# A decoder step with paged decode attention: decay rows over 128 partitions, a new token's decay as a bias, copies before memsets, and the first product in two halves

## The reference

```python
c_all = jnp.cumsum(jnp.concatenate([past_logf, logf_new], axis=1), axis=1)
cq = c_all[:, past_len:]
s = jnp.einsum('bqhd,bkhd->bhqk', qi, k) * scale
s = s + ci[..., None] - ckt[:, :, None, :]          # + cq[t] - c[s], per head
s = jnp.where(k_pos[None, :] <= pi[:, None], s, MASK_VALUE)
p = jax.nn.softmax(s, axis=-1)
o = jnp.einsum('bhqk,bkhd->bqhd', p, v)
```

## Time and profile before

| | |
|---|---|
| three runs | 1964.43, 1966.2, 1970.72 us; median 1966.2 |
| the profiled execution | 1965.43 us, of which the span from first to last instruction is 1963.4 |
| granted TensorE clock, mean | 0.975 of full speed |
| busy, share of the span | PE 95%, PEld 87%, DVE 47%, ACT 35%, POOL 29% |
| stages | layer 0 from 0; prompt attention from about 1010; decode from 1128; last trunk from 1475 |
| the 16 DMA engines, mean over the span | 139 GB/s; in decode 388 to 394 GB/s |

### The profile page before, as it was taken

How to read it: one execution, slowest core, us unless ns; L and a number is a source line. 1 busy time by engine, 2 the same in 40 slices (tenths; PEclk the granted TensorE clock), 3 DMA queues, 4 the chain that set the end, 5 groups by cost and what they waited for, 6 DMA issues and landing times. The chain is left out here.

```text
span 1963.4 us, 39366 instructions
## 1 busy us (share of the span) xinstructions
PE 1857.2 (95%) x16353; PEld 1698.7 (87%) x16353; DVE 928.5 (47%) x1406; ACT 690.0 (35%) x1082; POOL 578.0 (29%) x275
## 2 busy tenths in 40 slices
PE   6999998999999999999979899888889999999998
PEld 5999997999999999999977666555549999999998
DVE  4757767355555500354648654433323455555000
ACT  4355455332222121355436643333323312212121
POOL 2323322243333433333346200000003333334332
PEclk9999999999999999999998899999889999999999
DMA  4232241222222333222243789999983222223322
GB/s 109 82 105 78 78 111 48 83 79 86 86 77 86 92 85 88 59 73 76 76 143 104 250 283 393 394 391 388 389 329 86 87 82 80 86 82 92 88 76 78
DMA packets 288853, 272.92 MB, mean 139 GB/s; under 512 B 19234, under 2 KB 249859, under 8 KB 288036
## 3 DMA queue, kind: packets, MB, share of 16 engines
q1 hardware_dynamic: 286740, 267.91, 42.3%
q10 hardware_dynamic: 1792, 1.44, 0.2%
q0 software_dynamic: 144, 1.05, 0.2%
HBM read 252.09 MB, written 14.08 MB: 136 GB/s over the span
## 5 line engine op out<-in xcount | busy, mean ns | idle before, releaser
L2033 POOL TENSOR_TENSOR a_wl<-a_wraw,a_wh 128x1024 fp32r<-128x1024 f32 (+2 forms) x91 | 233.8, 2569 | 410.6 <-ACT a_wh L1959 410.6
L2033 POOL TENSOR_TENSOR b_wl<-b_wraw,b_wh 128x1024 fp32r<-128x1024 f32 (+1 forms) x67 | 175.4, 2619 | 300.6 <-ACT b_wh L1959 300.6
L1915 PE MATMUL ps<-xh,a_wh 128*128 128x288 f32 x1104 | 238.1, 297 | 0.0
L1915 PE MATMUL ps<-xl,a_wh 128*128 128x288 f32 x1104 | 237.0, 296 | 0.0
L1915 PE MATMUL ps<-xh,a_wl 128*128 128x288 f32 x1104 | 236.7, 296 | 0.0
L1959 ACT ACTIVATE a_wh<-a_wraw 128x1024 fp32r<-128x1024 f32 (+2 forms) x91 | 100.6, 1106 | 338.8 <-PE ps L1915 319.0
L1959 ACT ACTIVATE b_wh<-b_wraw 128x1024 fp32r<-128x1024 f32 (+1 forms) x67 | 76.0, 1134 | 318.4 <-PE ps L1915 318.4
L1915 PEld LDWEIGHTS ps<-xh,a_wh 128*128 128x128 f32 x1104 | 177.1, 187 | 1.1 <-issue 0.2
L1915 PEld LDWEIGHTS ps<-xh,a_wl 128*128 128x128 f32 x1104 | 177.2, 187 | 0.6
L1915 PEld LDWEIGHTS ps<-xl,a_wh 128*128 128x128 f32 x1104 | 177.2, 187 | 0.6
L2051 DVE TENSOR_TENSOR xT<-xT,ps 128x576 f32<-128x576 f32 x32 | 24.1, 754 | 322.0 <-PE ps L1915 322.0
(11 more groups left out here) (347 smaller groups left out, 3863.0 us busy)
## 6 DMA issues: line engine op xcount, KB each, us to landing
sa_kp<-in_cache_k SPq DMA_DIRECT2D x128, 512.0 KB, 11.1
sa_vp<-in_cache_v SPq DMA_DIRECT2D x102, 512.0 KB, 14.6
a_wraw<-in_w_gate_up SPq DMA_DIRECT2D x44, 512.0 KB, 3.8
b_wraw<-in_w_gate_up SPq DMA_DIRECT2D x44, 512.0 KB, 3.7
a_wraw<-in_a_w_in SPq DMA_DIRECT2D x32, 512.0 KB, 4.2
a_wraw<-in_w_down SPq DMA_DIRECT2D x16, 704.0 KB, 4.7
xl_plain<-in_cache_v SPq DMA_DIRECT2D x22, 512.0 KB, 14.9
b_wraw<-in_w_down SPq DMA_DIRECT2D x16, 704.0 KB, 4.7
```

The source lines that it names most:

```text
L1915: mm = pe.matmul(ps[0:width(n), bank(n) + a, 0:HALF], wt[:, base(n) + t, 0:width(n)], ap[:, first + t, a * HALF:(a + 1) * HALF], start=kin ...
L2033: pool.tensor_tensor(part(wl, n), part(wraw, n), part(wh, n).bitcast(F32), ALU.subtract).then_inc(e["low"], 1)
```

## The change

1. **Decode, rows.** `neg_decay` becomes `[sequence*16+head, part, token]`, so that a sequence's 256 KB are one piece. One DMA lays it on 128 partitions of 512 tokens (partition = head*8 + part*4 + group). A new constant `c_rowsel` (256 KB, loaded into `pp` at the beginning of decode and rounded by ScalarE into `rowsel`) has for each group a 128 x 128 matrix that picks the rows of this group and head. The matmul L1502 has 128 partitions in place of 34.
2. **Decode, bias.** The new tokens' decay isn't a row of the matmul any more. It is stored once, unsplit, and loaded as a column for each sequence into `shift` (128 x 8) by eight DMAs of single elements (`load_shift`) in prompt attention at j = 6, between `parts(6)` and three key pages. `save` adds it as the bias of its activation, `tail` with a tensor_scalar, and the maximum of the tail is taken from the result. The memsets of the ones, of `rowl`, half of the split of the new decay (two small VectorE instructions) and the waits on them go.
3. **Prompt attention.** VectorE makes its two copies ahead of its two memsets. ScalarE alternates: query half, copy, query half, copy.
4. **Layer 0.** Chunk 4 goes to bank 2 and waits for `low` at 2. The first product is made by halves of the tokens: the 24 matmuls of the first half wait for three chunks, those of the second for five.

```diff
@@ FirstNorm.tensor
             if c == 4:
-                pe.wait_ge(self.low, 1)
+                pe.wait_ge(self.low, 2)
...
+    def bank(self, c):
+        return 2 * c if c < 4 else 2
@@ hgrn_layer, unit
                     if n == 0:
-                        pe.wait_ge(first.low, 5)
-                    for t in range(KD):
-                        for i, (wt, at) in enumerate(((wh, k.xh), (wh, k.xl), (wl, k.xh))):
-                            for a in range(2):
...
+                        pe.wait_ge(first.low, 3)
+                    for half in ((0,), (1,)) if n == 0 else ((0, 1),):
+                        if half == (1,):
+                            pe.wait_ge(first.low, 5)
+                        for t in range(KD):
+                            for i, (wt, at) in enumerate(((wh, k.xh), (wh, k.xl), (wl, k.xh))):
+                                for a in half:
...
@@ prompt_attention
                     if j == 6:
+                        past.load_shift(sp)
                         keypages.load_early(sp, 5, 8)
...
-                for a in range(2):
-                    query_high(0, a)
-                past.act_rows(act)
+                query_high(0, 0)
+                past.act_rows(act, 1)
+                query_high(0, 1)
+                past.act_rows(act, 3)
...
+                past.dve_rows(dve, 0)
+                past.dve_rows(dve, 2)
                 dve.memset(qb[DH:DH + 4, 0].bitcast(F32), 1.0).then_inc(ones[0], 1)
-                past.dve_rows(dve, 0)
                 dve.memset(kb[DH:DH + 4, 0].bitcast(F32), 1.0).then_inc(ones[0], 1)
-                past.dve_rows(dve, 2)
@@ PastDecay
+    def load_shift(self, sp):
+        sp.wait_ge(self.newstored, 32)
+        for c in range(4):
+            for a in range(2):
+                at = a * DH + c * 2 * NQ
+                sp.dma_start(self.shift[32 * c + 16 * a:32 * c + 16 * a + 16, :], self.k.new_decay[:, at:at + 2 * NQ].rearrange("b n -> n b"),
+                             allow_slow_non_contiguous=True).then_inc(self.shifted, 16)
@@ sample_attention, rows
-                    s = b % 2
-                    for part in range(2):
-                        sp.dma_start(rowr[part * BH:(part + 1) * BH, s, :].bitcast(F32), k.neg_decay[part, b * BH:(b + 1) * BH, :]
-                                     ).then_inc(rload[s], 16)
-                    new_row(b)
...
+                    sp.dma_start(rowr[:, b % 2, :].bitcast(F32), k.neg_decay[b * BH:(b + 1) * BH].rearrange("h s (g n) -> (h s g) n", g=G)
+                                 ).then_inc(rload[b % 2], 16)
...
-                sp.wait_ge(past.newstored, 32)
-                sp.wait_ge(e["cleared"], 1)
+                sp.dma_start(pp[:, 0:G, :], k.w["c_rowsel"]).then_inc(e["sel"], 16)
                 rows(0)
@@ sample_attention, scores
-                            pe.wait_ge(rload[s], b // 2 * 64 + 64)
-                            pe.wait_ge(e["ones"], 3)
+                            pe.wait_ge(rload[s], b // 2 * 16 + 16)
+                            pe.wait_ge(e["selected"], 1)
...
-                        pe.matmul(ps[:, group % 2, :], rowl[:, s, :], rowr[:, s, g * SEQ:(g + 1) * SEQ], start=True, stop=False,
+                        pe.matmul(ps[:, group % 2, :], rowsel[:, g, :], rowr[:, s, :], start=True, stop=False,
@@ sample_attention, scalar
-                    act.activation(pr[:, b % 2, g * SEQ:(g + 1) * SEQ], ps[:, group % 2, :], ACT.Copy).then_inc(e["saved"], 1)
+                    act.activation(pr[:, b % 2, g * SEQ:(g + 1) * SEQ], ps[:, group % 2, :], ACT.Identity, bias=past.shift[:, b:b + 1]
+                                   ).then_inc(e["saved"], 1)
...
+                act.wait_ge(past.shifted, 128)
...
+                    if n == 0:
+                        act.wait_ge(e["sel"], 16)
+                        act.activation(rowsel[:], pp[:, 0:G, :], ACT.Copy).then_inc(e["selected"], 1)
@@ sample_attention, vector
-                    dve.tensor_copy(stail[:], ring_bank(n)[:, 0:NQ]).then_inc(e["tailed"], 1)
-                    dve.tensor_reduce(mx[:, G:G + 1], ring_bank(n)[:, 0:NQ], AX.X, ALU.max).then_inc(e["tailed"], 1)
+                    dve.tensor_scalar(stail[:], ring_bank(n)[:, 0:NQ], past.shift[:, b:b + 1], None, ALU.add).then_inc(e["tailed"], 1)
+                    dve.wait_ge(e["tailed"], 2 * b + 1)
+                    dve.tensor_reduce(mx[:, G:G + 1], stail[:], AX.X, ALU.max).then_inc(e["tailed"], 1)
```

More of the change, by code:

```diff
@@ L1203, in room @@
         self.cum2, self.cnew = k.sb(st, "pd_cum", [P, 2, NQ]), k.sb(st, "pd_cnew", [P, 2, NQ])
[L1204 removed]
+        self.newparts = k.sb(st, "pd_newparts", [P, 2, NQ], F32R)
     def load(self, sp):
@@ L1253, in quarter, with act_rows @@
         return ap[:, g * SEQ:(g + 1) * SEQ]
[L1255 to L1259, removed]
+    def act_rows(self, act, g):
+        act.wait_ge(self.turned, g + 1)
+        dst, src = self.spread(g)
+        act.activation(dst, src, ACT.Copy).then_inc(self.arows, 1)
     def act_high(self, act, g):
@@ L1318, in dve_new @@
         dve.wait_ge(self.cum, 3)
-        for part in range(2):
[L1320 to L1324, removed]
+        dve.tensor_copy(self.newparts[:, 0, :], self.cnew[:, 1, :]).then_inc(self.newparted, 1)
+        dve.wait_ge(self.newparted, 1)
+        dve.tensor_tensor(self.newparts[:, 1, :], self.cnew[:, 1, :], self.newparts[:, 0, :].bitcast(F32), ALU.subtract
+                          ).then_inc(self.newparted, 1)
 def sample_attention(k, ks, qs, oT, past, keypages, valuepages, room):
@@ L1331, in sample_attention @@
     e = {n: k.sem("sa_" + n) for n in (
-        "const", "fixed", "ones", "cleared", "filled", "scored", "saved", "mx", "max", "exp", "sum", "inv", "queries", "tailed",
-        "vnew", "mixed", "om", "picked", "done", "newrows")}
+        "const", "fixed", "filled", "scored", "saved", "mx", "max", "exp", "sum", "inv", "queries", "tailed",
+        "vnew", "mixed", "om", "picked", "done", "newrows", "sel", "selected")}
     copied = {n: k.sem("sa_copied_" + n) for n in ("act", "dve")}
@@ L1619, in _ @@
                 act.wait_ge(past.headed, 16)
-                for s in range(2):
-                    act.activation(rowl[0:2 * BH, s], past.headrow, ACT.Copy).then_inc(e["fixed"], 1)
+                act.activation(rowl[:], past.headrow, ACT.Copy).then_inc(e["fixed"], 1)
+                act.wait_ge(past.shifted, 128)
                 for n in range(BLOCKS * NB + PROB_AT + 1):
@@ L1639, in _ @@
             def _(pool):
-                pool.memset(rown[2 * BH:2 * BH + 2].bitcast(F32), 1.0).then_inc(e["ones"], 1)
-                for s in range(2):
-                    pool.memset(rowr[2 * BH:2 * BH + 2, s].bitcast(F32), 1.0).then_inc(e["ones"], 1)
                 raw, high, low = (r[:, 0:KD, :] for r in k.ring)
@@ L1723, in _ @@
                         if n < 2:
-                            dve.wait_ge(e["fixed"], 3)
+                            dve.wait_ge(e["fixed"], 2)
                             queries(n)
@@ L2433, in program @@
                 row_stored = k.sem("rows_stored")
-                past = PastDecay(k, past_logf, room[:, D + 2 * P:], pages, room[0:2 * BH, D + P:D + 2 * P])
+                past = PastDecay(k, past_logf, room[:, D + 2 * P:], pages, room[0:2 * BH, D + P:D + 2 * P], gains["a_norm"])
                 heads = AttentionInputs(k, row_stored, past)
```

42 lines of the change are left out of this document (18 added, 24 removed).

## The result

Seven runs of the changed kernel gave a median of 1953.65 us (1951.08 to 1960.91), beside 1966.2 for the kernel before: ratio 0.9934, 95% interval 0.9916 to 0.9953, so 13.0 us. A second measurement of the same kernel, later, gave 1959.05 us in twelve runs (1952.39 to 1963.54) and 0.9955 (0.9940 to 0.9969), 8.8 us. The change makes the kernel faster; by how much is known to some 4 us. The profiled execution took 1951.08 us, with a span of 1949.3 (before: 1965.43 and 1963.4).

A forecast was written before the change was run, and what follows sets the result against it. It took TensorE to bound the products, waits between engines prompt attention, and held DMA engines decode; 9.6 + 0.9 + 1.2 + 3.4 = 15.1 us off 1965.4 gave 1950.3, with 0.8 for the median 1951.1 us, range 1944 to 1959.

The forecast's parts named there:

- The row load: Decode: rows on 2 x 16 partitions cost 1.9 us a sequence beyond their bytes; 9.6 us saved for b = 3 to 7.
- the rival on descriptors: Decode row loads: cost goes by descriptors, so 128 pieces are slower than before, 1990 us; chance 0.03.
- take over half of the saving: Decode rival: TensorE becomes the bound and half of the 9.6 us is lost, 1956 us; chance 0.12.
- Decode's beginning: First scores of decode: rows arrive at 1133.0, scores at 1133.3; 0.9 us gained.
- the half clock behind it: Transposes behind decode's first wait: a bound of 1.6 us more if their half clock goes; not in the sum.
- the load of b = 2: Decode: this row load falls before the DMA engines are the bound; taken as 0, at most another 2.3 us.
- Waits for keys: Decode: TensorE's waits for key pages would shrink from 30 to about 20 us.
- Layer 0: First product starts at 23.7, not 25.49, and runs at full clock; done at 30.2 instead of 33.6, 3.4 us gained.
- Prompt attention: Its beginning: sums start at 1016.6 instead of 1017.82, 1.2 us gained; up to 3 more if the half clock goes.
- the rival that I gave 0.04: Prompt attention: the shift loads hold up head pair 7; at 4 us lost, 1955 us; chance 0.04.
- my 1104.4: Prompt attention: when SP gets past shift loads, key pages and `decays(7)`, ahead of `parts(7)` at 1104.60; cost nothing.
- The sum: Whole kernel: 9.6 + 0.9 + 1.2 + 3.4 = 15.1 us gained, median 1951.1 us.

The follow-up runs named there:

- rows128_512b: The changed kernel with each 2 KB of decay rows cut into four 512 B pieces by gaps in DRAM, still on 128 partitions; 1954.34 us in one run.
- pages_last: Changed kernel, shift loads in SP's gaps, pair 5's parts ahead of stores and pages, early key pages 2, 3, 3 behind pairs 5, 6, 7; 1949.87 us.
- changed_again: The changed kernel once more, word for word, on the same chip beside pages_last; 1959.05 us, 0.9955 to the kernel before.
- no_decode: The kernel before with only the reordered prompt attention and the first product by halves, decode as before; 1963.91 us, 0.9979.
- pages_behind: The changed kernel with the last four key pages before decode issued behind the selection constant and first rows; 1955.75 us, 0.9933.

## Why the prediction was right, and where it wasn't

*The row load.* Right in cause, and near in size. I took 1.5 + 1.6 + 2.0 + 2.3 = 7.4 us for b = 3 to 6; from issue to issue it is 173.1 - 166.6 = 6.5. Behind the issue of b = 7 decode is 2.8 us shorter (105.98 and 103.13), where I had 2.2. The rows on 32 partitions apart show the cause, and rows128_512b puts the rival on descriptors out. TensorE didn't take over half of the saving either.

*Decode's beginning.* Undersized. From the first transposes to sequence 3's issue it is 66.4 us in place of 68.6, so 2.2, where I took 0.9. The wait itself shrank by 0.23 only: I had the arrival at 1133.0, 4.9 us behind the first transposes, and it came after 5.8. But the half clock behind it, which I kept as a bound, went (1.3 us). The other 0.7 us have no row. All of it is there when `rows(2)` is issued (31.4 us behind the first transposes before, 29.1 after), so the load of b = 2 gave nothing, as in the sum. Decode in all gave 11.55 against 10.5.

*Waits for keys.* I wrote that they would go from 30 to about 20 us; they are 25 to 30 in the traces with the new layout. The step that failed is that the saving would show as less idle time. From the issue of sequence 3's rows to that of sequence 7's, 6.5 us shorter, TensorE's idle time falls from 22.2 to 20.6 us and its busy time from 150.9 to 146.0. The time at half clock falls from 17 to 14 us, which is worth at most 1.7 us of busy time. What the other 3.2 us are stays open.

*Layer 0.* The step is right: the first product gets the full clock, and it is out at 30.1 to 31.2 in eleven traces against 33.6 in two, 2.5 to 3.5 us where I took 3.4. I took the start for 23.7; it was 24.51 here and 23.50 in pages_last. Here TensorE's 31 transposes ahead of it took 4.99 us, in the kernel before 3.93 from the same start, and I have no reason for it. The twelfth trace with the halves, changed_again, is the late one told above. At the last head the median of the same eleven is 301.4 against 304.1 in two: 2.7 us of the 3.4 are left. In the changed kernel's own trace it is 1.3; no_decode, with the same layer 0, has 2.6, so I take it for scatter.

*Prompt attention.* The 1.2 us came exactly (3.39 us to the sums in place of 4.57), and the half clock stayed, as in the sum. It was then lost again, by the rival that I gave 0.04: the shift loads hold up head pair 7. In the eight traces with the loads where the change puts them it waits 0.3 to 3.0 us (median 2.0), in the others with pages as before not at all. I had reckoned SP's time, and that held: the eight loads took 4.74 us in place of 3.9, but the parts of pair 6 were out 2.6 us sooner, and those of pair 7 at 1102.83, before my 1104.4. What I left out is the queue behind SP. The three pages used to be issued 7.4 us ahead of these parts, and now 3.7, and 1.5 MB at 407 GB/s take 3.9 by my estimate: the parts land when the pages have.

*The sum.* The typical pieces, 2.7 in layer 0, 1.2 - 2.0 in prompt attention and 11.5 in decode, make 13.4 us where I had 15.1. The times say 13.0 and 8.8. That the first median, 1953.65, lies within 3 us of my 1951.1 is in part luck: too little at decode's beginning and the loss at head pair 7, which I had at nothing, cancel in part, and the median of twelve more runs of the same kernel lies 5 us higher. That what layer 0 wins reaches the end is seen for both early parts together (no_decode, 4.1 us), not for the halves alone, since the scatter below is larger than they are.

## What to carry to other kernels

Where the DMA engines are the bound, look for stretches with full share and few GB/s: here a transfer of 256 KB to 2 x 16 neighbouring partitions cost 0.64 + 1.9 us, four times its bytes at 407 GB/s. Most of that fell on the pages beside it, and every fourth partition was as good as all 128. A DMA that costs nothing in the queue that issues it can still push a large transfer closer ahead of a small, urgent one; reckon the bytes in flight when the urgent one is issued. And when pages only change places ahead of one waiter or another, the gain is what the last of them leaves.

## What the runs showed of the hardware

The time from the last V of layer 0 to the gather runs the same code in every kernel and took 698.4 to 706.0 us. In the two that lie furthest apart, 7.4 of the 7.6 us arise in one place, between 318 and 385 us. TensorE stands with nothing to wait for that the profile shows ("issue") ahead of the small matmuls of the last head. In the longer case this stall is longer, and the granted clock is lower behind it, but also before it (0.50 from 318 to 320 us, 1.00 in the other). The first is no_decode, the second pages_behind:

```profile
323.85 0.46 PE L394 MATMUL ps<-hg_levels 128*32 128x64 f32 x14 [1.84 <-issue]
...
330.00:340.00 10.00, 9.29 (x92) 8.66 (x91) 5.54 (x15) 6.20 (x10) 0.00 (x0) 1.00 0.22 61
```

```profile
326.76 0.46 PE L395 MATMUL ps<-hg_levels 128*32 128x64 f32 x14 [3.55 <-issue]
...
330.00:340.00 10.00, 10.00 (x40) 6.84 (x41) 5.70 (x21) 3.66 (x7) 0.00 (x0) 0.58 0.03 9
```

From 385 us on the two run in step, 7.2 us apart. Why the instructions come late in some executions stays open, as does why the wait ahead of pair 5 is anything from 3.3 to 8.5 us. The two together are as large as the spread of 10 us and more between runs of one kernel. That they make it isn't shown, since only one run of each has a trace. A spread of this size hides whatever is worth 2 us.
